# Column strips for the head, gates, energies and logits of a two-part transformer kernel, with its inputs queued between weight chunks

## The chip, the cores and the metric

The kernel runs on one core of a Trainium2 chip. The metric is the device time of one execution in microseconds (us). Everything is computed in 32-bit floats; the later layers use 32-bit products made of a high and a low part.

## What is computed

The reference takes 256 latent tokens `x` and 256 context tokens `ctx` of width 1024, and runs one block with a three-branch mixer and 16 experts, then four transformer layers. What the change touches lies in the first block:

```python
mod_l = jnp.split((jax.nn.silu(c) @ ada_w[l] + ada_b[l])[:, None, :], 6, axis=-1)
zc = modulate(rmsnorm(ctx, norm1_w[l]), mod_c[0], mod_c[1]) @ w_in[l] + b_in[l]
zl = modulate(rmsnorm(x, norm1_w[l]), mod_l[0], mod_l[1]) @ w_in[l] + b_in[l]
...
k = k * lax.rsqrt(jnp.sum(k * k, axis=0, keepdims=True) + EPS)      # filter energies
...
g_logits = (t @ lp["moe_rg_w"] + lp["moe_rg_b"]).astype(jnp.float32)
p_top, g_sel = lax.top_k(jax.nn.softmax(g_logits, axis=-1), 1)
e_logits = (t @ lp["moe_re_w"] + lp["moe_re_b"]).astype(jnp.float32).reshape(B * L, MOE_GROUPS, MOE_PER_GROUP)
...
a = jax.nn.silu(hg) * hu * combine[..., None].astype(t.dtype)
```

The slice `zc[..., OFF_MLG:OFF_GATE]` (and that of `zl`) of 16 columns holds the input and forget gates of the mLSTM branch.

## The kernel before

The order of the work is written out by hand for each engine; semaphores join the engines.

**Weights.** SyncE streams all weights through `ring`, 12 slots of 512 KB. Up to the experts they come as 31 chunks of four slots (2 MB), of which three fit; a chunk's load waits until `chunk_used` says that the chunk three earlier is done (L333). The signal rides on the first matmul after the chunk's last one (`used`). From the experts on (unit `split0`) they come as pairs of slots (1 MB), and each unit is split into `high` (ScalarE, L1143) and `low` (VectorE, L1592) before TensorE takes it; `split_to(n)` is the loop that does this up to unit n, and it stands in the order of both engines.

**Head.** ScalarE's queue loads `vecs`, `consts`, `xt` (the latents) and `ctx`, beside SyncE's chunks 0 to 2 and nine small loads of GpSimd. `ada(j)` multiplies one chunk of `ada_w` by the conditioning vectors in four column strips: weight tile k of 8 goes to the 32 output rows of strip k mod 4, so four matmuls of 32 columns each stand side by side in the array; `mod_out` copies the result to SBUF and `fold_columns` adds the four strips with a matmul against `fold`. Between `ada(1)` and `ada(2)` the mean square of all 512 tokens is taken with eight full matmuls (`mean_w`); VectorE forms the inverse root (L1598 to L1604) and scales both halves (L1606); `mods_ready` then lets ScalarE apply the modulation (L1172), and `in_values(0)` starts the projections. `in_values(s)` for s = 0 to 3 are the four value tiles, `in_keys(i)` the keys. Chunk 4 holds the value weights.

**Gates.** After `in_values(3)` the 16 gate columns are made for four token tiles, each with eight matmuls that stream 16 columns, and one for the bias. ScalarE copies them to `zp`, and after `in_keys(0)` TensorE turns them.

**Filter energies.** `energy(o)` for o = 0, 1 sums the squared filter taps with 16 matmuls of one column; VectorE takes them in `energy_eps`.

**Logits and expert 0.** After the second norm (`x_ready`) two token tiles of 20 logits are made with 18 matmuls. VectorE routes (L1982 to L2010; `first_hot` runs three times), then splits units 4 to 10, then makes expert 0's `hidden` (L2024), for which ScalarE's silu (L1425) is needed. TensorE runs `ffn_up(0)` meanwhile; `ffn_up(1)` waits for `h_raw`.

A matmul with 32-bit operands stands as two MATMUL records in the trace: eight matmuls are x16 there, and as x8 in the order rows below.

## Time and profile before

| What | us |
|---|---|
| median of three runs (2325.89 to 2328.65) | 2326.47 |
| the profiled execution, its own time | 2323.77 |
| its span on the core | 2322.0 |
| TensorE busy | 2149.4 (93%) |
| VectorE, ScalarE, GpSimd busy | 1280.7, 919.2, 109.0 |

### The profile page before, as it was taken

To read this page: it belongs to the slowest core of one execution; us is meant where nothing else is said; L and a number is where in the kernel's file an instruction comes from. 1 tells how busy PE (TensorE), PEld (TensorE's weight loads), DVE (VectorE), ACT (ScalarE), POOL (GpSimd) and SP (SyncE) were. 2 spreads that over 40 slices of the span, in tenths; PEclk is the share of its full clock that TensorE was granted. 3 is DMA by queue.
4 is the path that set the end of the run, shared out by engine and by line. 5 is a ranking of instruction groups with operands and counts; after the bars stand their busy time and mean duration, and the time that the engine had idled before them with its cause. 6 is when DMAs were issued, how large, how long until landed. Compare 5 with 4: busy or idle time off the path is not lost.

```text
span 2322.0 us, 27972 instructions
## 1 busy us (share of the span) xinstructions
PE 2149.4 (93%) x11510; PEld 1732.2 (75%) x11510; DVE 1280.7 (55%) x1903; ACT 919.2 (40%) x1448; POOL 109.0 (5%) x115
## 2 busy tenths in 40 slices
PE   4998999998999998899999998999998999988997
PEld 1556867775788877688799887788787788766886
DVE  1263742325555566555568676655576755656554
ACT  1123432003444435344345544444355444354442
POOL 1000000000000001000001012100001000020000
PEclk8799989998999999999999999999999999989999
DMA  7213334533454542345544332455543554424551
GB/s 291 85 66 152 122 140 147 194 137 117 162 181 181 182 164 108 136 181 183 173 182 171 128 126 93 145 183 182 179 146 128 181 181 181 163 94 152 181 181 73
DMA packets 47102, 357.23 MB, mean 154 GB/s; under 512 B 5370, under 2 KB 5557, under 8 KB 9664
## 3 DMA queue, kind: packets, MB, share of 16 engines
q1 hardware_dynamic: 41616, 334.51, 40.0%
q0 software_dynamic: 4784, 18.38, 2.3%
q10 hardware_dynamic: 576, 2.55, 0.3%
q8 instruction: 91, 1.49, 0.3%
q14 instruction: 35, 0.29, 0.0%
HBM read 354.38 MB, written 1.05 MB: 153 GB/s over the span
## 4 chain that ended last, share of the span: by engine, by line
PE 83%; DVE 10%; ACT 3%; issue 2%; DMA 1%; POOL 0%; ACTq 0%; DVEq 0%
PE pg L435 53%; PE pd L435 23%; PE pm L435 4%; DMA rh<-in_ctx 1%; PE pm L866 1%; DVE low L1592 1%; DVE small L1889 1%; DVE rs L1925 1%; DVE rs L1924 1%; DVE rs L1885 1%; DVE ar L2101 1%; DVE ar L1683 1%; ACT ar L1483 1%; PE pm L1008 1%; DVE xs L1935 0%
## 5 line engine op out<-in xcount | busy, mean ns | idle before, releaser
L1592 DVE TENSOR_TENSOR low<-ring,high 128x1024 fp32r<-128x1024 f32 x512 | 622.9, 1236 | 356.9 <-ACT high L1143 356.7
L435 PE MATMUL pg<-high,xs 128*128 128x512 f32 (+1 forms) x2496 | 749.6, 378 | 29.5 <-DVE xs L1935 14.3
L1143 ACT CAST high<-ring 128x1024 fp32r<-128x1024 f32 x512 | 525.1, 1048 | 372.7 <-PE pd L435 163.9
L435 PEld LDWEIGHTS pg<-high,xs 128*128 128x128 f32 x2496 | 464.2, 194 | 118.3 <-issue 21.3
L435 PE MATMUL pg<-low,xs 128*128 128x512 f32 (+1 forms) x1248 | 467.5, 375 | 0.0
L435 PE MATMUL pd<-high,hid 128*128 128x512 f32 x960 | 311.7, 396 | 7.0 <-DVE hid L2016 7.0
L435 PEld LDWEIGHTS pg<-low,xs 128*128 128x128 f32 x1248 | 242.5, 194 | 40.7
L435 PE MATMUL pg<-xs,high 128*128 128x256 f32 x1344 | 242.1, 283 | 0.0
L435 PEld LDWEIGHTS pd<-high,hid 128*128 128x128 f32 x960 | 180.7, 188 | 50.5 <-DVE hid L2016 8.2
L435 PEld LDWEIGHTS pg<-xs,high 128*128 128x128 f32 x1344 | 206.3, 188 | 5.0 <-issue 4.7
L435 PE MATMUL pg<-rh,ring 128*128 128x256 f32 (+1 forms) x832 | 207.4, 409 | 0.0
L435 PEld LDWEIGHTS pg<-rh,ring 128*128 128x128 f32 x832 | 161.3, 196 | 45.6 <-issue 25.3
L435 PE MATMUL pd<-low,hid 128*128 128x512 f32 x480 | 189.5, 395 | 0.0
L435 PE MATMUL pg<-xs,low 128*128 128x256 f32 x672 | 189.1, 281 | 0.0
L435 PEld LDWEIGHTS pg<-xs,low 128*128 128x128 f32 x672 | 126.5, 188 | 0.0
L435 PEld LDWEIGHTS pd<-low,hid 128*128 128x128 f32 x480 | 90.3, 188 | 20.9
L361 POOL TENSOR_TENSOR ar<-ar,small 128x256 f32<-128x256 f32 (+1 forms) x64 | 82.8, 1322 | 437.0 <-DVE small L2127 437.0
L2016 DVE TENSOR_TENSOR hid<-pm,hid 128x512 fp32r<-128x512 f32 x60 | 41.4, 691 | 93.6 <-ACT hid L1416 93.6
L1416 ACT CAST hid<-pm 128x512 fp32r<-128x512 f32 x60 | 35.2, 587 | 125.3 <-PE pm L866 125.3
L1483 ACT ACTIVATE ar<-ar,small 128x257 f32<-128x257 f32 (+5 forms) x128 | 67.0, 525 | 40.6 <-DVE small L2121 29.2
L1425 ACT ACTIVATE ar<-pg 128x256 f32<-128x256 f32 x120 | 46.2, 386 | 85.1 <-PE pg L435 85.0
L2081 DVE TENSOR_TENSOR ar<-ar,ropes 128x512 f32<-128x512 f32 x42 | 37.0, 880 | 68.4 <-ACT ar L1462 42.5
(322 smaller groups left out, 2048.9 us busy)
## 6 DMA issues: line engine op xcount, KB each, us to landing
ring<-in_wstream SPq DMA_DIRECT2D x256, 1024.0 KB, 4.8
ring<-in_wstream SPq DMA_DIRECT2D x31, 2048.0 KB, 7.8
gb<-in_long_rows POOLq DMA_DIRECT2D x21, 512.0 KB, 4.3
hdec<-in_hy_decay POOLq DMA_DIRECT2D x4, 512.0 KB, 4.4
rh<-in_xt ACTq DMA_DIRECT2D x1, 1024.0 KB, 23.1
rh<-in_ctx ACTq DMA_DIRECT2D x1, 1024.0 KB, 27.9
cx<-in_cx_tables POOLq DMA_DIRECT2D x1, 1024.0 KB, 5.1
cx<-in_dft_tables POOLq DMA_DIRECT2D x1, 1024.0 KB, 8.5
```

The source lines that it names most:

```text
L361: last = gp.tensor_tensor(w, w, smx[:, b, 2, t, 2 * p:2 * p + 2].unsqueeze(2).to_broadcast([P, 2, n]), ALU.mult)
L435: ins = nc.tensor.matmul(dst, lhs, rhs, start=start, stop=stop, skip_group_check=skip)
L866: last = nc.tensor.transpose(pm[u % 2][:, i * T + t * P:i * T + (t + 1) * P], hidden[:, t, i * P:(i + 1) * P], ident)
L1008: nc.tensor.transpose(pm[i][:, 0:P], scores(q, 0)[:, h, g * P:(g + 1) * P], ident)
L1143: nc.scalar.copy(high[:, (s - split0) % NHIGH, :], ring[:, s % NRAW, :]).then_inc(S("high_done"), 1)
L1416: nc.scalar.copy(hid[:, u % 2, 0, :, :], pm[u % 2][:, :].rearrange("p (i t) -> p i t", t=T)).then_inc(S("hid_high"), 1)
L1425: nc.scalar.activation(silu_g[:, t, :], pg[t][:, 0:T], ACT.Silu).then_inc(S("silu_done"), 1)
L1483: last = nc.scalar.activation(s, s, ACT.Exp, bias=smx[:, b, 0, t, h:h + 1], accum_out=smx[:, b, 1, t, h:h + 1])
L1592: V.tensor_tensor(low[:, s % NRAW, :], ring[:, s % NRAW, :], high[:, (s - split0) % NHIGH, :].bitcast(F32), ALU.subtract).then_inc(S("low_ ...
L1683: last = V.scalar_tensor_tensor(d, src, w[i], d, ALU.mult, ALU.add)
L2016: V.tensor_tensor(hid[:, u % 2, 1, :, :], pm[u % 2][:, :].rearrange("p (i t) -> p i t", t=T), hid[:, u % 2, 0, :, :].bitcast(F32), ALU.sub ...
L2081: V.tensor_tensor(rt[:, 0, :, :], raw[:, e % 2, :, :], cos.unsqueeze(1).to_broadcast([P, 2, T]), ALU.mult)
```

## The change

- **Input order.** The latents are loaded on SyncE's queue behind chunk 0, the context behind chunk 1, instead of on ScalarE's queue beside the chunks.
- **Head.** The mean squares are made by half, each in column strips (`square_strips`) and then folded by two full matmuls (`square_mean`) from a copy in SBUF; the latents' squares go to VectorE. The inverse root of each half is formed by itself, the latents' first; the context is scaled only after the modulation is ready. `ada(2)` and `ada(3)` write other PSUM banks. GpSimd sets the constants before its loads.
- **Gates, energies, logits.** The 128-token side is streamed (512 or 256 columns) and the narrow weights stand in four strips; ScalarE copies the result to SBUF (gates and logits with their bias), and a few narrow matmuls against `fold` add the strips and turn them. Between strips and fold other work is placed: `in_values(3)`, `in_pair("g", 0)`, `in_pair("g", 3)`, the first unit of `ffn_up(0)`.
- **Routing.** `first_hot` takes four VectorE instructions instead of eleven, with a constant `rank`.
- **Splits.** VectorE's split of the first four expert units stands ahead of the second norm instead of behind it; `hidden` and silu of expert 0 come after the split of unit 5 instead of unit 10.

```diff
+                if c == 0:
+                    sp.dma_start(rh[:, 0:2048], a["xt"]).then_inc(S("x_loaded"), 16)
+                elif c == 1:
+                    sp.dma_start(rh[:, 2048:4096], a["ctx"]).then_inc(S("ctx_loaded"), 16)
...
-            pe.wait_ge(S("consts_loaded"), 16)
+            def square_strips(half):
+
+                pe.wait_ge(S(("lat_sq", "ctx_sq")[half]), 1)
+                for k in range(KT):
+                    g = k % 4
+                    last = mm(pd[32 * g:32 * g + 32, 2, half * T:(half + 1) * T], ones[:, 0:32], sq2[:, half, k, :],
+                              k < 4, k >= 4)
+                last.then_inc(S("var_strips"), 1)
+
+            def square_mean(half):
+
+                pe.wait_ge(S("var_rows"), half + 1)
+                mm(pm[1][:, half * T:half * T + P], mean_w[:, :], nrm[:, 2, half * T:half * T + P], True, True)
+                mm(pm[1][:, half * T + P:(half + 1) * T], mean_w[:, :], nrm[:, 2, half * T + P:(half + 1) * T], True, True
+                   ).then_inc(S("nrm_var"), 1)
+
             pe.wait_ge(S("c_silu"), 1)
             ada(0, pg[0])
+            pe.wait_ge(S("ones_set"), 1)
+            square_strips(0)
             ada(1, pg[1])
+            square_mean(0)
+            pe.wait_ge(S("consts_loaded"), 16)
             fold_columns(0, pm[0][:, 0:8])
-            pe.wait_ge(S("constants"), 1)
-            pe.wait_ge(S("nrm_sq"), 2)
-            for k in range(KT):
-                last = mm(pm[1][:, :], mean_w[:, :], sq2[:, :, k, :], k == 0, k == KT - 1)
-            last.then_inc(S("nrm_var"), 1)
-            ada(2, pg[0])
+            square_strips(1)
+            ada(2, pd[:, 0, :])
+            square_mean(1)
             fold_columns(1, pm[0][:, 8:16])
-            pe.wait_ge(S("mod_row"), 2)
-            ada(3, pg[1])
+            ada(3, pd[:, 1, :])
             fold_columns(2, pm[0][:, 16:24])
             fold_columns(3, pm[0][:, 24:32])
+            pe.wait_ge(S("constants"), 1)
...
             mm(pm[1][0:64, 0:T], hyw[0:33, 0:64], feat, True, True).then_inc(S("hy_net"), 1)
             in_values(2)
+            for k in range(KT):
+                g = k % 4
+                last = mm(pm[0][32 * g:32 * g + 32, :], wg32[:, k, :], hc[:, :, k, :], k < 4, k >= 4)
+            last.then_inc(S("gate_strips"), 1)
             in_values(3)
+            pe.wait_ge(S("gates_copied"), 1)
             for s in range(4):
-                for k in range(KT):
-                    mm(pm[0][:, s * 16:(s + 1) * 16], hc[:, s // 2, k, (s % 2) * P:(s % 2 + 1) * P], wg16[:, k, :], k == 0, False)
-                last = mm(pm[0][:, s * 16:(s + 1) * 16], ones[0:1, :], row("b_gates", 0, 16), False, True)
+                last = mm(pm[0][:, s * 16:(s + 1) * 16], gate_rows[:, s * P:(s + 1) * P], fold[:, 0:16], True, True)
             last.then_inc(S("gates_raw"), 1)
...
                 pe.wait_ge(S("hy_tapsq"), o + 1)
+                if o:
+                    pe.wait_ge(S("hy_eps"), o)
+                for i in range(4):
+                    last = mm(pm[0][32 * i:32 * i + 32, :], ones[:, 0:32], hdec[:, i // 2, (i % 2) * DB:(i % 2 + 1) * DB],
+                              True, True)
+                last.then_inc(S("hy_energy"), 1)
+
+            def energy_columns(o):
+
+                pe.wait_ge(S("energy_copied"), o + 1)
                 for c in range(BT):
-                    for i in range(4):
-                        last = mm(pm[0][:, 4 * o + c:4 * o + c + 1],
-                                  hdec[:, i // 2, (i % 2) * DB + c * P:(i % 2) * DB + (c + 1) * P],
-                                  ones[:, 0:1], i == 0, i == 3)
-                last.then_inc(S("hy_energy"), 1)
+                    last = mm(pm[0][:, 4 * o + c:4 * o + c + 1], energy_rows[:, c * P:(c + 1) * P], fold[:, 0:1], True, True)
+                last.then_inc(S("hy_energies"), 1)
 
             def spectrum(o):
...
-            last.then_inc(S("logits"), 1)
+            for k in range(KT):
+                g = k % 4
+                last = mm(pm[0][32 * g:32 * g + 32, 0:T], wr32[:, k, :], h1[:, k, :], k < 4, k >= 4)
+            last.then_inc(S("logit_strips"), 1)
+
+            def logit_columns():
+
+                pe.wait_ge(S("logits_copied"), 1)
+                for s in range(TT):
+                    last = mm(pm[0][:, s * 20:(s + 1) * 20], logit_rows[:, s * P:(s + 1) * P], fold[:, 0:20], True, True)
+                last.then_inc(S("logits"), 1)
 
             def weights(n):
...
-                    ffn_up(u0, range(4))
+                    ffn_up(u0, (0,))
+                    logit_columns()
+                    ffn_up(u0, (1, 2, 3))
                 else:
...
+            def norm_root(half):
+
+                act.wait_ge(S("nrm_eps"), half + 1)
+                cols = slice(half * T, (half + 1) * T)
+                nc.scalar.activation(nrm[:, 1, cols], nrm[:, 0, cols], ACT.Sqrt).then_inc(S("nrm_root"), 1)
+
+            mod_out(0)
+            mod_out(1)
+            norm_root(0)
+            act.wait_ge(S("ctx_loaded"), 16)
+            nc.scalar.activation(sq2[:, 1, :, :], hc[:, 1, :, :], ACT.Square).then_inc(S("ctx_sq"), 1)
+            mod_out(2)
+            norm_root(1)
...
+            act.wait_ge(S("gate_strips"), 1)
+            nc.scalar.activation(gate_rows[:, :], pm[0][:, :], ACT.Identity, bias=vec("b_gates")
+                                 ).then_inc(S("gates_copied"), 1)
             take_values(3)
...
+            act.wait_ge(S("logit_strips"), 1)
+            nc.scalar.activation(logit_rows, pm[0][:, 0:T], ACT.Identity, bias=vec("b_route")
+                                 ).then_inc(S("logits_copied"), 1)
             act.wait_ge(S("group_diff"), 1)
...
-                    last.then_inc(S("nrm_scaled"), 1)
-            then(last)
+            dve.wait_ge(S("x_loaded"), 16)
+            V.tensor_tensor(sq2[:, 0, :, :], hc[:, 0, :, :], hc[:, 0, :, :], ALU.mult).then_inc(S("lat_sq"), 1)
+
+            def norm_rows(half):
+
+                cols = slice(half * T, (half + 1) * T)
+                dve.wait_ge(S("var_strips"), half + 1)
+                V.tensor_copy(nrm[:, 2, cols], pd[:, 2, cols]).then_inc(S("var_rows"), 1)
+                dve.wait_ge(S("nrm_var"), half + 1)
+                V.tensor_scalar(nrm[:, 0, cols], pm[1][:, cols], EPS_RMS, None, ALU.add).then_inc(S("nrm_eps"), 1)
+
+            def norm_scale(half):
+
+                cols = slice(half * T, (half + 1) * T)
+                dve.wait_ge(S("nrm_root"), half + 1)
+                y, v, t = (nrm[:, i, cols] for i in (1, 0, 2))
+                then(V.reciprocal(y, y))
+                then(V.scalar_tensor_tensor(t, y, -0.5, y, ALU.mult, ALU.mult))
+                then(V.tensor_tensor(t, t, v, ALU.mult))
+                then(V.scalar_tensor_tensor(y, t, 1.5, y, ALU.add, ALU.mult))
+                return V.tensor_tensor(hc[:, half, :, :], hc[:, half, :, :], y.unsqueeze(1).to_broadcast([P, KT, T]), ALU.mult)
+
+            norm_rows(0)
+            norm_scale(0).then_inc(S("nrm_scaled"), 1)
+            norm_rows(1)
...
+            dve.wait_ge(S("ctx_loaded"), 16)
+            then(norm_scale(1))
             for k in range(KT):
...
+            split_to(split0 + 3)
             dve.wait_ge(S("x_landed"), 16)
             for c in range(2):
...
             low_part(1, 0)
             normalised(1, 1)
             low_part(1, 1)
-            split_to(split0 + 3)
...
-                then(V.tensor_copy(seen, dst[:, :, 0:1]))
-                for j in range(1, 4):
-                    then(V.tensor_scalar(free, seen, -1.0, 1.0, ALU.mult, ALU.add))
-                    then(V.tensor_tensor(seen, seen, dst[:, :, j:j + 1], ALU.max))
-                    then(V.tensor_tensor(dst[:, :, j:j + 1], dst[:, :, j:j + 1], free, ALU.mult))
+                then(V.tensor_tensor(ranked, dst, rank.unsqueeze(1).to_broadcast([P, 2, 4]), ALU.mult))
+                then(V.tensor_reduce(seen, ranked, AX, ALU.max))
+                then(V.tensor_tensor(dst, ranked, wide(seen), ALU.is_equal))
 
             dve.wait_ge(S("logits"), 1)
             then(V.tensor_copy(R[:, 0:40], pm[0][:, 0:40]))
...
-                    first_by_tile = by_tile and u == u0
-                    if first_by_tile:
-                        hidden_raw(u, 0)
+                    if u == u0:
+                        if by_tile:
+                            hidden_raw(u, 0)
                         split_to(UP[u] + 5)
-                        hidden_raw(u, 1)
+                        for t in range(int(by_tile), TT):
+                            hidden_raw(u, t)
                     split_to(UP[u] + 8)
                     if u > u0:
                         hidden_low(u - 1)
                     split_to(UP[u] + 10)
-                    if not first_by_tile:
+                    if u > u0:
                         for t in range(TT):
                             hidden_raw(u, t)
                 last = u0 + n - 1
```

Three places show how the order moves. First TensorE's head, up to the first two value tiles (`pg`, `pd` and `pm` are PSUM, `rs` the squares, `rh` the tokens, `nrm` the rows of the norm). Before:

```order
L435 MATMUL pg<-ring,cs 32x512 x16
L435 MATMUL pm<-consts,mod_row 128x2 x4
L435 MATMUL pm<-rs,mean_w 128x512 x8
L435 MATMUL pg<-ring,cs 32x512 x8
L435 MATMUL pm<-consts,mod_row 128x2 x4
L435 MATMUL pg<-ring,cs 32x512 x8
L435 MATMUL pm<-consts,mod_row 128x2 x8
L435 MATMUL pg<-ring,rh 128x512 x8
```

Now:

```order
L443 MATMUL pg<-ring,cs 32x512 x8
L443 MATMUL pd<-rs,ones 32x256 x8
L443 MATMUL pg<-ring,cs 32x512 x8
L443 MATMUL pm<-nrm,mean_w 128x128 x2
L443 MATMUL pm<-consts,mod_row 128x2 x4
L443 MATMUL pd<-rs,ones 32x256 x8
L443 MATMUL pd<-ring,cs 32x512 x8
L443 MATMUL pm<-nrm,mean_w 128x128 x2
L443 MATMUL pm<-consts,mod_row 128x2 x4
L443 MATMUL pd<-ring,cs 32x512 x8
L443 MATMUL pm<-consts,mod_row 128x2 x8
L443 MATMUL pg<-ring,rh 128x512 x8
```

The latents' squares now come between the first two chunks of `ada_w`, and the eight full matmuls of 512 columns are gone.

Second, TensorE's gates, behind the third value tile (`wg` and `ar` the gate weights). Before:

```order
L435 MATMUL pg<-ring,rh 128x512 x8
L435 MATMUL pg<-rows,ones 128x512
L435 MATMUL pm<-wg,rh 128x16 x8
L435 MATMUL pm<-rows,ones 128x16
...
L435 MATMUL pm<-ar 64x256
L435 MATMUL pg<-rh,ring 128x512 x8
L435 MATMUL pm<-consts,zp 8x128 x16
```

Now:

```order
L443 MATMUL pm<-rh,ar 32x512 x8
L443 MATMUL pg<-ring,rh 128x512 x8
L443 MATMUL pg<-rows,ones 128x512
L443 MATMUL pm<-consts,gate_rows 128x16 x4
L443 MATMUL pm<-ar 64x256
L443 MATMUL pg<-rh,ring 128x512 x8
L443 MATMUL pm<-consts,zp 8x128 x16
```

Of 36 narrow matmuls in one place, 8 in strips stand ahead of the fourth value tile and 4 narrow ones behind it.

Third, VectorE between the routing and expert 1 (`low` is a split, `ar<-ar,pg` the hidden tile, `hid` its low part). Before:

```order
L1592 TENSOR_TENSOR low<-ring,high 128x1024 [waits high_done,combine]
L1592 TENSOR_TENSOR low<-ring,high 128x1024 [waits high_done] x6
L2024 SCALAR_TENSOR_TENSOR ar<-ar,pg 128x256 [waits silu_done] x2
L1592 TENSOR_TENSOR low<-ring,high 128x1024 [waits high_done] x2
L2016 TENSOR_TENSOR hid<-pm,hid 128x512 [waits hid_high]
```

Now:

```order
L1654 TENSOR_TENSOR low<-ring,high 128x1024 [waits high_done,combine]
L1654 TENSOR_TENSOR low<-ring,high 128x1024 [waits high_done]
L2097 SCALAR_TENSOR_TENSOR ar<-ar,pg 128x256 [waits silu_done] x2
L1654 TENSOR_TENSOR low<-ring,high 128x1024 [waits high_done] x7
L2089 TENSOR_TENSOR hid<-pm,hid 128x512 [waits hid_high]
```

Five splits have gone from ahead of the hidden tile to behind it.

## Rows read from the trace of the kernel before

**Rows 1.** The page: the chain that ended last, by engine.
```profile
PE 83%; DVE 10%; ACT 3%; issue 2%; DMA 1%; POOL 0%; ACTq 0%; DVEq 0%
```

**Rows 2.** Chain that ended last, to the first projection: start us, us, what.
```profile
2.14 27.92 DMA rh<-in_ctx
30.08 3.71 ACT rs L1153 x2
...
50.41 3.36 DVE nrm L1601
...
58.19 2.30 DVE rh L1606
...
61.95 18.05 PE pg L435 x36
```

**Rows 3.** Stretches: length, PE, PEld, DVE, ACT, POOL busy, PEclk, DMA share, GB/s.
```profile
4.00:14.00 10.00, 0.00 (x0) 0.00 (x0) 0.00 (x0) 0.92 (x2) 2.86 (x10) 1.00 1.02 416
66.00:96.00 30.00, 30.00 (x69) 12.08 (x68) 4.75 (x14) 3.98 (x6) 1.59 (x3) 1.00 0.19 70
97.00:111.00 14.00, 14.00 (x74) 13.49 (x73) 0.00 (x0) 0.78 (x5) 0.00 (x0) 0.60 0.43 151
558.00:570.00 12.00, 12.00 (x45) 10.95 (x46) 7.55 (x26) 0.27 (x2) 0.00 (x0) 0.50 0.48 176
```

**Rows 4.** TensorE in order of time, modulation chunks: start us, us, tiles, count.
```profile
16.73 5.81 PE L435 MATMUL pg<-ring,cs 128*32 128x512 f32 x32 [16.73 <-DMA consts<-in_consts]
...
167.44 1.92 PE L435 MATMUL pm<-ring,cs 128*32 128x512 f32 x16
169.30 7.17 PE L435 MATMUL pg<-rh,ring 128*128 128x256 f32 x32
...
195.15 3.64 PE L435 MATMUL pm<-ring,cs 128*32 128x512 f32 x16
```

**Rows 5.** TensorE in order of time, gates and the work around them.
```profile
80.50 7.13 PE L435 MATMUL pg<-ring,rh 128*128 128x512 f32 x16
...
96.73 1.96 PE L435 MATMUL pm<-wg,rh 128*128 128x16 f32 x16
...
111.53 9.71 PE L435 MATMUL pg<-rh,ring 128*128 128x512 f32 x16
121.16 3.66 PE L435 MATMUL pm<-consts,zp 128*8 128x128 f32 x32
```

**Rows 6.** TensorE in order of time, the two filter energies.
```profile
308.14 6.99 PE L435 MATMUL pm<-ones,hdec 128*128 128x1 f32 x32 [2.73 <-ACT hdec L1332]
...
316.69 9.54 PE L435 MATMUL pg<-rh,ring 128*128 128x256 f32 x32
326.07 8.75 PE L435 MATMUL pd<-hk,cx 128*128 128x512 f32 x20
...
355.24 3.63 PE L435 MATMUL pm<-ones,hdec 128*128 128x1 f32 x32
...
369.31 8.75 PE L435 MATMUL pd<-hk,cx 128*128 128x512 f32 x20
```

**Rows 7.** TensorE in order of time, logits and the first expert.
```profile
557.54 3.60 PE L435 MATMUL pm<-wr,ar 128*128 128x20 f32 x16 [4.18 <-DVE xs L1935]
...
585.70 0.80 PE L435 MATMUL pg<-high,xs 128*128 128x512 f32 x1 [6.32 <-DVE ar L2024]
```

**Rows 8.** Chain that ended last, in expert 1: start us, us, what.
```profile
594.49 5.57 PE pg L435 x24
```

**Rows 9.** VectorE in order of time, routing and the first hidden tiles.
```profile
565.79 0.20 DVE L1982 COPY ar<-pm 128x40 f32<-128x40 f32 x1 [3.77 <-PE pm L435]
...
577.22 8.04 DVE L1592 TENSOR_TENSOR low<-ring,high 128x1024 fp32r<-128x1024 f32 x7
585.17 0.87 DVE L2024 SCALAR_TENSOR_TENSOR ar<-ar,pg 128x256 f32<-128x256 f32 x2
```

**Rows 10.** ScalarE in order of time, the same place.
```profile
581.93 1.28 ACT L1425 ACT_TABLE_LOAD   x1
```

More of the change, by code:

```diff
@@ L469, in fold_columns @@
                 for i in range(4):
[L470 removed]
+                    last = mm(dst[:, 2 * i:2 * i + 2], mod_row[:, j % 2, i * P:(i + 1) * P], fold[:, 0:2], True, True)
                 last.then_inc(S("mod_folded"), 1)
@@ L2282, in constants @@
     put("flip", np.eye(P)[::-1])
-    fold = np.zeros((P, 2))
-    for g in range(4):
-        fold[32 * g, 0] = fold[32 * g + 1, 1] = 1.0
-    put("fold", fold)
+    put("fold", np.tile(np.eye(32), (4, 1)))
+    put("rank", np.tile(np.arange(4, 0, -1), (P, 1)))
     ch = 2 * np.pi * np.outer(p, p) / P
```

94 lines of the change are left out of this document (41 added, 53 removed).

## The prediction

> **What bounds the kernel now.** I read the page first, then the chain that ended last, then TensorE in order of time at the places that the change touches. The chain is TensorE for 83% of the span [rows 1], so a microsecond taken out of TensorE's own queue is a microsecond of the span, wherever no other engine is about to finish later. The change touches four places, all before expert 1.
>
> *Head.* The first projection starts at 61.95 [rows 2]. Up to there the chain is no work of TensorE: the context lands at 30.1 (27.9 after its issue), both halves are squared (1.85 each), the root of 512 columns is inverted (3.36), both halves are scaled (2.30 each) [rows 2]. In that time the DMA engines move 416 GB/s [rows 3]: the inputs are late because they share the engines with three, in the end four, 2 MB chunks.
>
> *Gates.* From 96.73 to 121.16 TensorE makes the gates, a small matmul and `in_keys(0)`: 24.4 us [rows 5]. Of it 13.8 are the gates, 72 records that stream 16 columns. They begin at 0.12 each and end at 0.22, the granted clock of the stretch is 0.60 [rows 3], and `in_keys(0)` takes 9.71 where such a block takes 7.13 at full pace [rows 5]: the narrow matmuls are paid twice.
>
> *Energies.* The same: the 32 one-column records of the first energy take 6.99, 0.22 each, the pace at which the gates ended, and the pair behind it 9.54; the whole from 308.14 to `spectrum(0)` at 326.07 is 17.9. The second, 355.24 to 369.31, is 14.1 [rows 6].
>
> *Logits and expert 0.* `x_ready` comes at 557.5; the logits take 8.1 at 0.50 [rows 3, 7]; VectorE then routes for 11.4 (565.79 to 577.22), splits seven units (8.0) and makes the hidden tile, and `ffn_up(1)` starts at 585.70 after an idle 6.3 [rows 7, 9]. Its first records are slow again (0.80 for the first [rows 7]); later ones take 5.57 for 24, 0.23 each [rows 8].
>
> **The price of a strip block.** `ada` is one already: 16 records of 512 columns start at 167.44 and the next work at 169.30, 1.86 in all; at half clock 3.64 [rows 4]. So eight matmuls of 512 columns cost 1.86 at 2.4 GHz, about 3.6 at 1.2; four cost 0.93; eight of 256 columns 0.93 and 1.8. A fold is eight narrow records of 0.12, 0.95; at half clock 1.9 [rows 5].
>
> **Head, step by step.** On SyncE's queue the order is now chunk 0, `xt`, chunk 1, `ctx`, chunk 2. I take the measured 416 GB/s from 2 us on, 1.0 MB for the small loads, and first come first served within the queue: `xt` is complete at 12 (4.1 MB), chunk 1 at 17, `ctx` at 20, chunk 2 at 25, chunk 3 at 30, chunk 4 (the value weights) at 35 (13.6 MB). `chunk_used` is now raised by the square strips and means, but each comes at least 4 us before the queue runs dry, so no load waits.
> TensorE at half clock, as before at the start: `ada(0)` 10 to 13.6; VectorE squares the latents from 12 to 14.3 (2.3, the scaling's row), strips to 16.5; `ada(1)` 17.4 to 21; mean, eps, then ScalarE's table load (1.28 [rows 10]) and root to 23.3; ScalarE squares the context (1.85) to 25.2; strips to 27, `ada(2)` to 30.5. VectorE scales the latents from 23.4 (1.7 for 256 columns instead of 3.36, three short steps, 2.3) to 28.7, under that. Mean and fold to 33, `ada(3)` to 36.7, copy, two folds, the modulation's small steps: the first projection at 41.5. With all behind 27 at full clock it is 35.5, and then chunk 4 (35) is as late. I take 40, near the slow end, since TensorE idles or runs narrow folds for about a third of this time: **22 less** (bounds 14 and 26.5).
> A rule of the skill gives the input order another price. The Trainium skill, "DMA: Bandwidth & Descriptors", section "Queues, rings and completion order", says that each DMA engine takes the queues in turn, packet by packet; with equal turns the context, 2.6 MB deep in its own queue, would have come at about 15 and the move behind chunk 1 would delay it by 5. The row says 30.1, so the sum goes by the row.
>
> **Gates.** Strips 1.86, folds 0.95, the small matmul 0.57, `in_keys(0)` 7.13: 10.5 for 24.4. ScalarE's copy is covered by `in_values(3)` (8 us); without that cover it would cost 0.6. **13.9 less**; at half clock throughout 8.
>
> **Energies.** Strips 0.93, the narrow fold of `fold_columns` 0.95, the pair 7.1, the new fold 0.95: 9.9 for 17.9. But TensorE still idles 2.7 before it [rows 6], so I leave 1.8 of half pace in: 6.2 less (bounds 3 and 8). Second: 0.93, `ada(8)` 1.9, pair 7.1, 0.95 for 14.1: 3.2 less (0 and 3.5). VectorE now gets its energies a pair later and is held there in `energy_eps`; behind it wait `add_columns` and the next convolution. `ada(7)`, which needs the former, comes only after `spectrum(0)` (8.75), so this costs nothing. **9.4 less.**
>
> **Logits and expert 0.** From `x_ready`: strips at half clock 1.8, the first unit's 12 records at twice 0.23, 5.2 (I take 5.1), folds 0.5, logits ready at 7.5 (now 8.2). Routing loses 21 of its 57 instructions, each 0.20 (11.43 / 57): 7.3 for 11.4, to 14.9. Two splits of 1.2 instead of seven (8.04 / 7 = 1.15), hidden tile 0.45: `ffn_up(1)` at 17.8, where now it is 28.2. TensorE itself is through `ffn_up(0)` at 15.7 (36 more records of 0.23), and ScalarE's silu, behind two casts (2.1) and the table load (1.28), comes at 16.7, just under VectorE. So it idles 2.1 instead of 6.3 and should keep its pace, some ten records at 0.23 saved, 2.3 more. The four splits put ahead of the norm fall into idle time of VectorE; the 4.6 they took ran beside the logits. **12.7 less** (9 and 14).
>
> **Sum.** 22 + 13.9 + 9.4 + 12.7 = 58. Nothing behind expert 1 is touched and DMA is far from full there, so all of it shows: span 2322.0 - 58 = 2264.0, with the 1.8 outside the span 2265.8; the median of the runs is 2.7 above the profiled execution, so **2268.5**. Bounds: 14 + 8 + 3 + 9 = 34 less (2292) and 26.5 + 13.9 + 11.5 + 14 = 66 less (2260).
>
> **Rivals.**
> - *All at full pace* (0.15): the denser head rouses the clock from `ada(2)` on, the idle before the energy costs nothing. Head 26.5, energies 11.5: 65 less, **2262**. Against it, each idle of over 2 us so far was followed by slow matmuls.
> - *The hand-offs decide the head* (0.18): each half now goes TensorE, VectorE, TensorE, VectorE, ScalarE, VectorE in turn, and one late step (the copy for the second mean waits behind the scaling of the latents) pushes `ada(3)` and all after it. First projection at 50: **2279**.
> - *The clock stays low at the new places* (0.11): gates save 8, energies 3, the expert 5: 38 less, **2288**.
> - *Strips don't stand side by side* (0.04): each record costs its full 0.43. Gates +5, energies +5, logits +5, squares +10: **2293**. The `ada` rows speak against it. A switch of the array's form could also cost by itself: the Trainium skill, "TensorEngine Tiling (Array Packing)", section "Key Properties", says that changing the tiling mode drains the engine. It gives no price; the `ada` row holds both of its switches, 0.15 over four groups of 0.43, so six new blocks pay 1 us by the row, and the prices above have it in.
> - *Slower* (0.01): the half clock of the start lasts through the projections, because the head's dense matmuls of 512 columns are replaced by strips and idle between them. A block of 7.1 us then takes 14.2; from the ninth such block on the gain of 58 is gone, and nine make 2268.5 + 64 = **2332**. Against it, the projections that start at 61.95, after a head in which VectorE alone works for ten microseconds, are at clock 1.00 from 66 on [rows 2, 3].
>
> **How the numbers follow.** The forecast has 0.51. The range may leave out at most 0.2: it drops the three dearest cases (0.16 together), holds the hand-off case at 2279 with some room, and at the low end the full-pace case at 2262 with five for what the four prices may add up to beyond it: 2257 to 2285. A measurement tells about 0.2% (4.7 us) from no change; every case but the last is more than six times that below 2326.5: faster 0.98, same 0.01, slower 0.01.
>
> **What would show it.** In the changed profile: first projection near 40; gates, strips to `zp` without the value tile, about 10.5, at clock 1.00; `in_keys(0)` at 7.1; `spectrum(0)` 10 to 12 after the energy's start; `ffn_up(1)` 18 after the second norm, with an idle of 2. I am wrong in the head if `ctx` lands after 25 or the first projection comes after 45, and in the rest if the small folds alone pull the clock down, or if a new wait on `energy_copied`, `gates_copied` or `logits_copied` stands in TensorE's list.

## The result and the profile after

| | before | after |
|---|---|---|
| median of the runs, us | 2327.39 (2325.89 to 2328.65, 4 runs) | 2267.98 (2265.89 to 2268.92, 4 runs) |
| the profiled execution: own time, span | 2323.77, 2322.0 | 2268.92, 2267.1 |

The ratio is 0.9744, 95% interval 0.9727 to 0.9761: 59.4 us or 2.6% faster. Predicted were 2268.5 with a range of 2257 to 2285. The same pair was timed again for e12 below: 2265.65 against 2319.04, ratio 0.977 (0.9752 to 0.9789), 53.4 us. So the changed kernel repeats to 2.3 us, and the kernel before moved by 8.4: the gain is 53 to 59 us.

The page of the changed kernel, the engines' busy time and the chain by engine:

```profile
PE 2121.1 (94%) x11438; PEld 1701.7 (75%) x11438; DVE 1281.1 (57%) x1890; ACT 920.1 (41%) x1452; POOL 109.2 (5%) x115
...
PE 85%; DVE 9%; ACT 3%; issue 1%; DMA 1%; POOL 0%; SPq 0%; DVEq 0%; ACTq 0%
```

Beside [rows 1], TensorE has 85% of the chain instead of 83%, and of its busy time 28 us have gone. To see where the time went I read the same marks in both traces, the start of a stage on TensorE, in us:

| mark | before | after | less by then |
|---|---|---|---|
| first projection | 62.0 | 39.4 | 22.6 |
| gates turned (`zp`) | 121.2 | 84.4 | 36.8 |
| first energy | 308.1 | 271.1 | 37.0 |
| `spectrum(0)` | 326.1 | 284.1 | 42.0 |
| `spectrum(1)` | 369.3 | 324.0 | 45.3 |
| logits | 557.5 | 514.0 | 43.5 |
| expert 0's hidden tile turned | 593.9 | 537.1 | 56.8 |
| end of the span | 2322.0 | 2267.1 | 54.9 |

The stretch of the last line but one to the end, 1728 us, holds nothing that the change touches. Over the fourteen profiled executions of this study it lasted 1722 to 1732 us, and the edits below don't touch it either, so the total of one execution carries several microseconds of scatter that a mark does not. I read the experiments by the marks up to the turned hidden tile. A mark comes from one execution, though, and two stretches ahead of that tile also vary where no edit touches them: from the first projection to `zp` 45.0 or 46.8 to 48.2 us, and from the logits to the turned tile 21.6 to 21.8 or 23.0 to 23.1 (see the last section).

**Head.** TensorE in order of time (start, us, operation, tiles, counts, idle before and its releaser), to be held against [rows 2]:

```profile
9.71 3.64 PE L443 MATMUL pg<-ring,cs 128*32 128x512 f32 x16 [9.71 <-ACT cs L1191]
15.46 1.94 PE L443 MATMUL pd<-rs,ones 128*32 128x256 f32 x16 [2.10 <-DVE rs L1660]
19.81 3.64 PE L443 MATMUL pg<-ring,cs 128*32 128x512 f32 x16 [2.41 <-DMA ring<-in_wstream]
...
27.68 1.93 PE L443 MATMUL pd<-rs,ones 128*32 128x256 f32 x16 [1.58 <-ACT rs L1212]
29.39 3.29 PE L443 MATMUL pd<-ring,cs 128*32 128x512 f32 x16
...
34.04 1.92 PE L443 MATMUL pd<-ring,cs 128*32 128x512 f32 x16
...
39.39 2.90 PE L443 MATMUL pg<-ring,rh 128*128 128x512 f32 x3 [1.55 <-ACT rh L1220]
```

The context no longer decides. TensorE starts at 9.7 instead of 16.7, since it no longer waits for `consts` ahead of `ada(0)`, and then waits 2.1 us for the latents' squares, 2.4 for chunk 1, 1.6 for the context's squares and 1.6 for the modulation. The last of the four `ada` chunks is the first at full pace (1.92 for 16 records, before it 3.64, 3.64, 3.29).

**Gates.** The same view, in answer to [rows 5]:

```profile
65.79 1.92 PE L443 MATMUL pm<-rh,ar 128*32 128x512 f32 x16
67.64 7.13 PE L443 MATMUL pg<-ring,rh 128*128 128x512 f32 x16
...
75.76 1.06 PE L443 MATMUL pm<-consts,gate_rows 128*128 128x16 f32 x8
...
77.32 7.13 PE L443 MATMUL pg<-rh,ring 128*128 128x512 f32 x16
84.39 3.66 PE L443 MATMUL pm<-consts,zp 128*8 128x128 f32 x32
```

**Energies.** Both up to their spectra, in answer to [rows 6]:

```profile
271.10 1.94 PE L443 MATMUL pm<-hdec,ones 128*32 128x512 f32 x8 [2.73 <-ACT hdec L1383]
272.96 1.87 PE L443 MATMUL pm<-consts,mod_row 128*128 128x2 f32 x8
274.69 8.76 PE L443 MATMUL pg<-rh,ring 128*128 128x256 f32 x32
...
284.10 8.83 PE L443 MATMUL pd<-hk,cx 128*128 128x512 f32 x20
...
313.44 1.06 PE L443 MATMUL pm<-hdec,ones 128*32 128x512 f32 x8
...
323.97 6.25 PE L443 MATMUL pd<-hk,cx 128*128 128x512 f32 x14
```

**Logits and expert 0.** TensorE, in answer to [rows 7], then VectorE, in answer to [rows 9]:

```profile
513.99 1.93 PE L443 MATMUL pm<-ar,wr 128*32 128x256 f32 x16 [4.18 <-DVE xs L2010]
...
520.76 0.52 PE L443 MATMUL pm<-consts,ar 128*128 128x20 f32 x4
...
531.37 0.50 PE L443 MATMUL pg<-high,xs 128*128 128x512 f32 x1 [1.64 <-DVE ar L2097]
```

```profile
521.31 0.20 DVE L2055 COPY ar<-pm 128x40 f32<-128x40 f32 x1 [7.38 <-PE pm L443]
...
528.57 2.36 DVE L1654 TENSOR_TENSOR low<-ring,high 128x1024 fp32r<-128x1024 f32 x2
530.84 0.87 DVE L2097 SCALAR_TENSOR_TENSOR ar<-ar,pg 128x256 f32<-128x256 f32 x2
```

From the logits' first record to `ffn_up(1)` it is 17.4 us instead of 28.2, and the idle before it 1.64 instead of 6.32. VectorE has two splits (2.36) between the routing and the hidden tile, not seven. The stretches of the places above, with the columns of [rows 3]:

```profile
4.00:14.00 10.00, 3.64 (x16) 0.59 (x16) 0.98 (x1) 0.80 (x2) 2.62 (x8) 1.00 1.02 378
66.00:76.00 10.00, 10.00 (x36) 3.76 (x29) 0.00 (x0) 1.61 (x4) 0.00 (x0) 1.00 0.01 2
272.00:284.00 12.00, 12.00 (x56) 9.76 (x48) 2.37 (x4) 2.38 (x4) 1.14 (x2) 0.75 0.68 264
516.00:528.00 12.00, 12.00 (x46) 9.68 (x47) 5.55 (x35) 3.53 (x6) 0.00 (x0) 0.82 0.68 252
```

The gates now run at 1.00 where [rows 3] had 0.60. At the energy and the logits part of the slow clock has stayed (0.75 and 0.82).

### The profile page after: what moved, and what is told of

It is laid out like the page before. It is cut to its first block, busy times and chain, and to the rows that moved or that the text cites. A ratio compares the mean times of both kernels' runs of the same rounds, so it can differ in the third digit from the quotient of the medians.

```text
span 2267.1 us, 27822 instructions
## 1 busy us (share of the span) xinstructions
PE 2121.1 (94%) x11438; PEld 1701.7 (75%) x11438; DVE 1281.1 (57%) x1890; ACT 920.1 (41%) x1452; POOL 109.2 (5%) x115
## 4 chain that ended last, share of the span: by engine, by line
PE 85%; DVE 9%; ACT 3%; issue 1%; DMA 1%; POOL 0%; SPq 0%; DVEq 0%; ACTq 0%
PE pg L443 55%; PE pd L443 24%; PE pm L443 2%; PE pm L908 1%; DVE small L1964 1%; DVE low L1654 1%; DMA ring<-in_wstream 1%; DVE rs L2000 1%; DVE rs L1999 1%; DVE rs L1960 1%; DVE ar L2175 1%; DVE ar L1758 1%; ACT ar L1545 1%; PE pm L1052 1%; DVE xs L2010 1%
## 5 line engine op out<-in xcount | busy, mean ns | idle before, releaser
L1545 ACT ACTIVATE ar<-ar,small 128x257 f32<-128x257 f32 (+5 forms) x128 | 67.0, 525 | 41.5 <-DVE small L2195 30.1
L1486 ACT ACTIVATE ar<-pg 128x256 f32<-128x256 f32 x120 | 46.2, 386 | 84.5 <-PE pg L443 84.4
```

The lines of the kernel that those rows point to most:

```text
L1486: nc.scalar.activation(silu_g[:, t, :], pg[t][:, 0:T], ACT.Silu).then_inc(S("silu_done"), 1)
L1545: last = nc.scalar.activation(s, s, ACT.Exp, bias=smx[:, b, 0, t, h:h + 1], accum_out=smx[:, b, 1, t, h:h + 1])
```

## The experiments

Twelve kernels ran, in three groups, each on one chip with the kernel before beside them. The medians of before were 2320.7 in the first group (e1 to e4), 2325.2 in the second (e5 to e8) and 2319.0 in the third (e9 to e12). Only the third group holds the changed kernel (e12). For e2 to e8 the cost against the changed kernel is therefore read from marks: their medians lie 4.4 to 10.6 us above 2267.98, their ratios 0.0033 to 0.0073 above 0.9744 (7.7 to 17 us), and the base that moved by 8 us makes both rough.

The theory is the prediction's: four separate gains, the head's in the waits ahead of the first projection, the others in TensorE's own queue, with the clock as a good part of them at the gates, the energies and the expert. The rivals stand with each run: that one part of the head is the whole of it, or that narrow matmuls cost what they cost for another reason.

### The head: order alone, split alone

e1 puts only the input order into the kernel before; e2 takes only the order out of the changed kernel.

```diff
+                if c == 0:
+                    sp.dma_start(rh[:, 0:2048], a["xt"]).then_inc(S("x_loaded"), 16)
+                elif c == 1:
+                    sp.dma_start(rh[:, 2048:4096], a["ctx"]).then_inc(S("x_loaded"), 16)
...
-            act.dma_start(rh[:, 0:2048], a["xt"]).then_inc(S("x_loaded"), 16)
-            act.dma_start(rh[:, 2048:4096], a["ctx"]).then_inc(S("x_loaded"), 16)
```

> The kernel before with one edit: latents and context on SyncE's queue behind chunks 0 and 1, head and all else as before. Theory A (late inputs are half of the head's cost, the whole-width norm the other half): context at 20 instead of 30.1, squares to 24.4, the eight full matmuls to 34, then 16 us of norm as before: first projection at about 50 instead of 61.95, the kernel 12 us faster than before (2315). Theory B (the order of the inputs is the whole of the head's gain): first projection near 40, 22 us faster. Theory C (the split norm is the whole of it): within 3 us of before.

> The changed kernel with the two input loads back on ScalarE's queue beside the chunks; everything else as changed. Theory A: the latents land at 22 instead of 13, TensorE stands at the square strips behind ada(0), ada(1) starts at 26 instead of 19.8, first projection at about 46 instead of 39.4: 6.5 us slower than the changed kernel (4 to 10). Theory B: 20 us or more slower. Theory C: no difference.

e1: 2313.85 us (2309.23 to 2321.71, 10 runs), ratio 0.9969 (0.9949 to 0.9989). Its chain that ended last begins with the context, which lands at 21.9 instead of 30.1 (start, us, what):

```profile
2.12 19.79 DMA rh<-in_ctx
...
21.93 3.71 ACT rs L1155 x2
...
52.72 7.47 PE pg L439 x10
```

The first projection comes at 52.7, 9.2 earlier than before. Of it 8.2 is the context's landing. Theory A had said 50 and 12 us: its parts are right, its size was too large, and by medians e1 is only 6.9 us under before. Theories B (40) and C (within 3 us) are out.

e2: 2275.62 us (2274.08 to 2276.76, 4 runs), ratio 0.9799 (0.9767 to 0.983). TensorE's head:

```profile
26.86 1.93 PE L439 MATMUL pd<-rs,ones 128*32 128x256 f32 x16 [13.91 <-DVE rs L1658]
...
46.33 8.80 PE L439 MATMUL pg<-ring,rh 128*128 128x512 f32 x16 [1.55 <-ACT rh L1218]
```

Now the latents land at 24.4, and TensorE idles 13.9 us for their squares. The first projection comes at 46.3, 6.9 later than in the changed kernel (expected: 6.5). So of the head's 22.6 the order is worth 9.2 in the old head and 6.9 in the new one, and all the rest together 13.4 to 15.7: neither is the whole. This rest is the split norm with its strips, the squares on VectorE, the two other PSUM banks, and `ada(0)` without the wait for `consts`; these were not taken apart. Both loads stood in ScalarE's queue behind 0.46 MB of `vecs` and `consts`. The latents landed 22.7 us after their issue and the context 24.4 after its own, but `consts`, ahead of both, had itself taken 14.4.

The Trainium skill, "DMA: Bandwidth & Descriptors", section "Queues, rings and completion order", has each DMA engine take the queues in turn, packet by packet. The prediction's estimate of 15 us from it, for data 2.6 MB deep, takes turns of equal size. The packets are not equal: ScalarE's queue moved its first 0.47 MB in 288 packets, SyncE's has 8 KB in each. An estimate from the same rule with turns of one packet is about 22 us for the context: its 576 packets (2.6 MB), as many of SyncE's (4.6 MB) and 1.0 MB of small loads at 416 GB/s. It landed at 30.1 in [rows 2] and at 26.5 here, so neither estimate agrees.

### The gates: back, and spread

e3 makes the gates as before, 72 narrow records behind `in_values(3)`. e4 makes the same records, but one token tile behind each of the four value tiles (`gate_tile(s)` is the loop of before for tile s). In both, ScalarE's copy for the strips is gone.

```diff
...
             in_values(0)
+            gate_tile(0)
             in_values(1)
+            gate_tile(1)
...
             in_values(2)
-            for k in range(KT):
-                g = k % 4
-                last = mm(pm[0][32 * g:32 * g + 32, :], wg32[:, k, :], hc[:, :, k, :], k < 4, k >= 4)
-            last.then_inc(S("gate_strips"), 1)
+            gate_tile(2)
             in_values(3)
...
+            gate_tile(3).then_inc(S("gates_raw"), 1)
```

> The changed kernel with the gates as before: 72 narrow records in one place behind the fourth value tile, nothing else undone. Theory A: 14 us slower than the changed kernel (2282), the narrow matmuls falling to 0.22 each and in_keys(0) at 9 to 10 us. Theory B (the gain at the gates was the earlier context or another piece of the head): under 5 us.

> As the one before, but each token tile's 18 narrow records stand behind its own value tile instead of all 72 together. Same matmuls, same number. Theory A (nearly half of the gates' cost was the fallen clock, which needs the narrow matmuls in a row): 0.12 each throughout, in_keys(0) at 7.1, so 72 x 0.12 = 8.8 for 2.8: 6 us slower than the changed kernel (2274), 8 us faster than with the gates in one place. Theory D (the cost belongs to the narrow matmuls wherever they stand): 14 us slower.

e3 (gates as before): 2278.55 us (2277.01 to 2284.85, 4 runs), ratio 0.9817 (0.9782 to 0.9851). From the first projection to `zp` it is 59.1 us instead of 45.0, 14.1 more. Six kernels that leave this part as it is (e2, e5 to e8, e11) took 46.8 to 48.2 for it, against which it is 10.9 to 12.3 more:

```profile
73.90 1.96 PE L443 MATMUL pm<-ar,rh 128*128 128x16 f32 x16
...
76.11 2.82 PE L443 MATMUL pm<-ar,rh 128*128 128x16 f32 x16
...
79.39 3.60 PE L443 MATMUL pm<-ar,rh 128*128 128x16 f32 x16
...
88.55 9.85 PE L443 MATMUL pg<-rh,ring 128*128 128x512 f32 x16
```

Sixteen narrow records take 1.96, then 2.82, then 3.60: the pace halves while they run, and `in_keys(0)` behind them pays 2.7. Theory B (under 5 us) is out.

e4: 2275.85 us (2272.2 to 2287.26, 4 runs), ratio 0.9808 (0.9768 to 0.9849). The same stretch takes 59.4. By this mark spreading gave nothing, and by medians 2.7 us, within the scatter of both:

```profile
58.94 1.96 PE L443 MATMUL pm<-ar,rh 128*128 128x16 f32 x16
...
61.72 8.83 PE L443 MATMUL pg<-ring,rh 128*128 128x512 f32 x16
...
71.53 2.17 PE L443 MATMUL pm<-ar,rh 128*128 128x16 f32 x16
...
74.17 9.99 PE L443 MATMUL pg<-ring,rh 128*128 128x512 f32 x16
...
88.78 9.51 PE L443 MATMUL pg<-rh,ring 128*128 128x512 f32 x16
```

The narrow records now stay near full pace (1.96 and 2.17 for 16), but from the second such run on the dense tile behind it loses: 8.83, 9.99 and 9.51 instead of 7.13, together 6.9 us, at a granted clock of 0.80, 0.71 and 0.74. The narrow records themselves, with their bias, cost 6.8 more than the strips and folds. So theory A's 6 us failed, and theory D's 14 held. Where it lies is new: here half of the loss falls on the dense work behind the narrow records. The first such run (at 48.6) cost nothing behind it. In strips, the 16 records of 512 columns (1.92) are followed by a value tile of 7.13 in all ten traces that have them. Behind the eight folds of 16 columns (1.06) `in_keys(0)` takes 7.13 in four of these and 8.56 to 8.83 in six, so up to 1.7 of e4's last 2.4 may not be the narrow records'.

### The energies back

`energy(o)` is one function for both energies. With it `energy_columns` and ScalarE's two copies go:

```diff
...
-                if o:
-                    pe.wait_ge(S("hy_eps"), o)
-                for i in range(4):
-                    last = mm(pm[0][32 * i:32 * i + 32, :], ones[:, 0:32], hdec[:, i // 2, (i % 2) * DB:(i % 2 + 1) * DB],
-                              True, True)
+                for c in range(BT):
+                    for i in range(4):
+                        last = mm(pm[0][:, 4 * o + c:4 * o + c + 1],
+                                  hdec[:, i // 2, (i % 2) * DB + c * P:(i % 2) * DB + (c + 1) * P],
+                                  ones[:, 0:1], i == 0, i == 3)
```

> The changed kernel with both filter energies as before: 32 one-column records each, no copy, no fold. Theory A: 4.9 + 3.5 = 8.5 us slower than the changed kernel, energy(0) to spectrum(0) back at about 18 us, energy(1) to spectrum(1) at 11 to 14. Theory B (the gain there is only the clock's phase): under 3 us.

e5: 2277.82 us (2274.54 to 2279.66, 4 runs), ratio 0.9796 (0.9773 to 0.9818). From the first energy to `spectrum(0)` 18.1 instead of 13.0, from the second to `spectrum(1)` 14.1 instead of 10.5: 8.6 in all, as expected (8.5), and theory B (under 3) is out. One thing goes the other way: the output projection, far behind both, takes 27.73 us here and 29.43 in the changed kernel, which leaves 6.9 net.

### Routing, hidden tile, logits, each back alone

e6 gives `first_hot` its eleven instructions back, e7 puts expert 0's silu and hidden tile behind unit 10, e8 makes the logits with 18 narrow matmuls ahead of the expert. Of e7, VectorE's list (ScalarE's silus move in the same way):

```diff
...
-                    if u == u0:
-                        if by_tile:
-                            hidden_raw(u, 0)
+                    if u == u0 and by_tile:
+                        hidden_raw(u, 0)
                         split_to(UP[u] + 5)
-                        for t in range(int(by_tile), TT):
-                            hidden_raw(u, t)
+                        hidden_raw(u, 1)
                     split_to(UP[u] + 8)
...
-                    if u > u0:
+                    if u > u0 or not by_tile:
```

> The changed kernel with first_hot as before, 21 more VectorE instructions of 0.20 in the routing. Theory A (VectorE's chain sets when expert 1 starts): 4.2 us later all through, TensorE's idle before ffn_up(1) 5.8 instead of 1.6, and as many as ten slow records behind it: 4 to 6.5 us slower. Theory E (TensorE and ScalarE's silu would have come as late anyway): under 1.5 us.

> The changed kernel with silu and hidden of expert 0 behind the split of unit 10 again. Theory A: five splits of 1.15 = 5.7 us ahead of the hidden tile, idle 7.4 before ffn_up(1), slow records behind it: 6 to 8 us slower. Theory E: under 1.5 us, since the splits are needed before long anyway.

> The changed kernel with the logits as before (36 narrow records in one place, VectorE's short routing and early hidden kept). Theory A: logits at 8.2 after the norm instead of 7.3, and TensorE through ffn_up(0) 6 us later (at 22 instead of 15.5), so TensorE becomes the later one and ffn_up(1) starts at 22 instead of 17.4: 4.5 us slower. Theory E (VectorE alone decides): 0.9 us slower.

`ffn_up(1)` in e6, then in e7; in the changed kernel the idle is 1.64 and the first record takes 0.50:

```profile
537.49 0.80 PE L443 MATMUL pg<-high,xs 128*128 128x512 f32 x1 [5.81 <-DVE ar L2099]
```

```profile
539.51 0.79 PE L443 MATMUL pg<-high,xs 128*128 128x512 f32 x1 [7.33 <-DVE ar L2095]
```

| | median, ratio | by marks |
|---|---|---|
| e6 | 2272.38 (2269.92 to 2277.7), 0.9777 (0.9753 to 0.9801) | `ffn_up(0)` to the turned tile 27.7 for 21.2: 6.5 |
| e7 | 2277.54 (2269.34 to 2281.34), 0.9791 (0.9763 to 0.982) | the same 28.6: 7.4 |
| e8 | 2273.91 (2271.91 to 2278.32), 0.9787 (0.9761 to 0.9812) | logits to the turned tile 27.4 for 23.1: 4.3 |

All three came as theory A had it (4 to 6.5, 6 to 8 and 4.5); theory E is out for each. The medians of e6 and e8 are 4.4 and 5.9 us above 2267.98, that of e7 9.6. Each can hold the 1.4 us by which the logits' stretch varies (last section), which changes none of these verdicts. Singly they cost 18.2, together they gave 13.3 (10.8 to `ffn_up(1)` and 2.5 behind it). They lie on the same chain, and the first two each make the idle long enough (5.8 and 7.3) for the slow first records (0.80 and 0.79 instead of 0.50) to come back.

### What the changed kernel left: two idles

The changed kernel still idles 2.73 us before the first energy (above), and 5.19 before the mLSTM's first scores, where all 28 records up to 162 run at half pace:

```profile
152.66 3.78 PE L443 MATMUL pd<-ar 128*128 128x256 f32 x8 [5.19 <-ACT ar L1305]
...
158.37 3.64 PE L443 MATMUL pm<-ring,cs 128*32 128x512 f32 x16
```

Both come from the order in which the engines' lists are written. e9 moves the first energy's strips behind the pair that followed them, and their fold behind `spectrum(0)`; ScalarE's copy and VectorE's `energy_eps(0)` move back with them. e10 moves ScalarE's three silus ahead of its copy of the output gate's pair, and the two for the keys wait for the second signal of the convolutions instead of the fourth. e11 does both; e12 is the changed kernel once more. TensorE's part of e9, then e10:

```diff
...
-            energy(0)
...
             in_pair("g", 0)
-            energy_columns(0)
+            energy(0)
             spectrum(0)
+            energy_columns(0)
```

```diff
...
             take_pair("o", 0)
+
+            act.wait_ge(S("conv_out"), 2)
+            nc.scalar.activation(kf, kf, ACT.Silu)
+            nc.scalar.activation(kc, kc, ACT.Silu)
+            act.wait_ge(S("conv_out"), 4)
+            nc.scalar.activation(qf, qf, ACT.Silu).then_inc(S("qk_silu"), 1)
             take_pair("o", 1)
-
-            act.wait_ge(S("conv_out"), 4)
-            nc.scalar.activation(qf, qf, ACT.Silu)
-            nc.scalar.activation(kf, kf, ACT.Silu)
-            nc.scalar.activation(kc, kc, ACT.Silu).then_inc(S("qk_silu"), 1)
```

> The changed kernel, with the first energy's strips moved two steps back in TensorE's order: the weights of the next half, the fold of chunk 6 and the pair before it stand ahead of them, so that ScalarE's squared taps (hdec), for which TensorE idled 2.73 us, are there when they are asked for. My theory: the idle of 2.7 goes, and with it the half clock that lasts 8.6 + 1.7 + 1.9 us behind it, of which about 3 us is loss: 5 to 6 us less than the changed kernel, and from the start of the first energy to spectrum(0) no record at half pace. Rival: the taps' chain through ScalarE and VectorE is what decides, and the wait only moves to the next hand-off (hy_eps before spectrum(0), or hy_energies): then the gain is 0 to 2 us, and an idle stands in front of spectrum(0) or the second taps.

> The changed kernel, with ScalarE's silu of the mLSTM's queries and keys moved ahead of its copy of the output gate's pair, in front of which it stands in no dependence. TensorE idled 5.2 us before the mLSTM's first scores, for these silus, and its first records after that were at half pace (about 3.8 us of loss). My theory: both go, 7 to 9 us less than the changed kernel. Rival: VectorE's convolution is the later of the two inputs of the silu; then moving the silu only moves ScalarE's own idle, and the gain is under 2 us.

> Both edits together on the changed kernel. My theory: they lie over 20 us apart and each removes an idle and the slow clock behind it, so they add: 12 to 15 us less than the changed kernel, about 2255 if it stands at 2268. Rival: a busier stretch is paid for by a slower clock elsewhere, so the sum is less than the two single gains by 3 us or more.

> The changed kernel once more, unchanged, in the same call as its three variants. It gives them their base, and it shows how much one part varies by itself: from the first projection to the turned gates the changed kernel took 45.0 us in its first profiled execution, and 46.8 to 48.2 in five variants that did not touch this part, with in_keys(0) at 8.6 to 8.8 us instead of 7.13. If that is variation from one execution to the next, this one may show 45 to 48; if the variants caused it, it shows 45.0 and in_keys(0) 7.13 again.

| | median of 4 runs, us | ratio to before | turned hidden tile at | against e12: mark, median |
|---|---|---|---|---|
| e12 | 2265.65 (2263.49 to 2267.73) | 0.977 (0.9752 to 0.9789) | 536.8 | |
| e9 | 2259.84 (2257.05 to 2260.86) | 0.974 (0.9724 to 0.9757) | 528.8 | -8.0, -5.8 |
| e10 | 2263.62 (2253.48 to 2271.33) | 0.9756 (0.9717 to 0.9795) | 527.3 | -9.5, -2.0 |
| e11 | 2251.15 (2247.47 to 2253.4) | 0.9703 (0.9685 to 0.9722) | 521.5 | -15.3, -14.5 |

e9, TensorE around the first energy:

```profile
270.06 7.17 PE L443 MATMUL pg<-rh,ring 128*128 128x256 f32 x32 [0.72 <-DMA ring<-in_wstream]
277.16 1.06 PE L443 MATMUL pm<-hdec,ones 128*32 128x512 f32 x8
278.15 8.85 PE L443 MATMUL pd<-hk,cx 128*128 128x512 f32 x20
286.84 0.95 PE L443 MATMUL pm<-consts,energy_rows 128*128 128x1 f32 x8
```

No record is slow, and the energy costs 1.06 and 0.95. What is late next is a transfer, 0.72 us of weights before the pair. From the taps' matmuls ahead of the first energy (255.7 in the changed kernel) to `spectrum(1)` it is 63.0 us against 68.3, 5.3 less, inside the 5 to 6 expected. The rest of the 8.0 came later: 1.7 in the output projection, which I had not foreseen, and 1.4 behind the logits. That 1.4 is no gain of this edit, since e2, e3 and e5, which leave both places alone, show it too.

e10, the same place as above:

```profile
147.61 1.89 PE L443 MATMUL pd<-ar 128*128 128x256 f32 x8
...
150.49 1.92 PE L443 MATMUL pm<-ring,cs 128*32 128x512 f32 x16
```

The idle is gone and every record is at full pace: from `zp` to the scores 5.4 less (62.9 against 68.3), from there to the filter taps 4.6 less, together somewhat more than the 7 to 9 expected. The mark at the turned tile says 9.5, the median only 2.0. The four runs do not agree among themselves (two near 2255, two near 2271) and only the first has a trace, so the silus' gain is shown up to the turned tile of that execution, and how much of it every execution keeps is open.

e11 is the fastest kernel of the study, 14.5 us under e12 and 3% under before. In the traces the two edits add: 5.4 and 4.6 at the silus, 5.7 at the energy and 1.7 in the output projection, as if each were alone. By medians 5.8 and 2.0 don't make 14.5, which is e10's scatter again.

e12 repeats the changed kernel's marks to within 0.3 us up to the turned tile, and then ends 5.4 earlier. From the first projection to `zp` it shows 45.0 us and `in_keys(0)` at 7.13, which both readings in its expectation allow. e9 and e10, at 45.0 and 45.1, speak against a variant as such being the cause of 46.8 to 48.2; it stays open.

## Why the prediction was right

The forecast case came in: 2267.98 against 2268.5. That the two agree to 0.5 us is luck. The span came 3.1 us longer than forecast (2267.1 against 2264.0), and the sum then added 2.7 because the median of before lay that much above its profiled execution; this time the median lies 0.9 below it. By terms, in the profiled executions:

| term | predicted | measured |
|---|---|---|
| head | 22 | 22.6 |
| gates | 13.9 | 14.2 |
| first energy | 6.2 | 4.9 |
| second energy | 3.2 | 3.5 |
| logits to `ffn_up(1)` | 10.4 | 10.8 |
| `ffn_up(1)` at full pace | 2.3 | 2.5 |
| parts that the sum left out | 0 | -3.6 |
| sum, span | 58 | 54.9 |

*Head.* Right in size, through two errors that cancel. Chunk 1 landed at 19.8, not 17: the stretch from 4 to 14 moved 378 GB/s, not the 416 that I took over from [rows 3], which accounts for 1 us of it. That put `ada(1)` 2.4 later and the context's squares after it. Against it `ada(3)` was already at full pace (1.92, not 3.6), where my 40 lay between the sum's two ends. The hand-off rival (2279) did not come: TensorE waits four times, three of them at a hand-off, but 1.6 to 2.4 us each, and `ada(3)` starts at 34.0 without a wait. e1 and e2 show that the order and the rest of the head both carry it.

*Gates.* As worked out: 1.92, 1.06, 0.64 and 7.13. ScalarE's copy is covered. e3 takes 14.1 back, 10.9 at the least. What the runs add is that spreading the narrow records doesn't keep the slow clock away (e4): half of their price was then paid by the tiles behind them. The prediction's sign of being wrong, small folds that alone pull the clock down, is neither met nor excluded: in six of ten traces `in_keys(0)` behind the folds lost 1.4 to 1.7, and in the same six the first value tile, after the head, had been slower too (8.80 to 10.1 against 8.59 to 8.67).

*Energies.* The term that was mis-sized: 9.4 forecast, 8.5 measured. I left 1.8 us of half pace behind the 2.7 idle. It was more: the strips took 1.94 for 0.93 to 1.06, the fold 1.87 for 0.95 and the pair 8.76 for 7.17, 3.4 us in all. The clock rose later than I took from the rows of before. In e9 the idle and the loss go together. e9 also moves the fold away, but at the silus e10 takes out only the idle, and the slow records behind it go too. With the 1.70 us of the output projection, which comes and goes with this edit (last section), the energies gave 6.8.

*Logits and expert 0.* Each step within 0.5 us of its place: strips 1.93 (1.8), logits ready at 7.3 (7.5), splits from 14.6 (14.9), `ffn_up(1)` at 17.4 (17.8), idle 1.64 (2.1). TensorE keeps its pace over this idle, as predicted, and does not over 5.8 (e6). That the four splits ahead of the norm cost nothing shows in the unchanged 4.18 before the logits.

*Parts that the sum left out.* I took nothing for them. The output projection's 64 records took 29.43 us, where before and in e9 they took 27.73. The remaining 1.9 lies in the scatter of the last 1728 us.

One reading of the prediction is wrong: not every idle of over 2 us was followed by slow matmuls. Before, the output projection started after an idle of 2.10 and ran at full pace, 27.73 for 64 records.

*The rivals.* Full pace everywhere (2262) was wrong at the energy and at the logits' first unit (clock 0.75 and 0.82). The clock staying low (2288) was wrong at the gates. Strips that don't stand side by side are excluded by 1.92 for 16 records of 512 columns (0.43 each would make 6.9), and a slow clock through the projections by the 7.13 at 67.64.

## What to carry to other kernels

A narrow matmul costs twice: a record of 16 columns took 0.12 us, as much as one of 512 columns does where four strips run side by side, and dense work behind such records ran at a lower clock. Turning the product round, so that the long side streams and the narrow weights stand in four column strips, took 14 of 24 us away (11 at the least), while spreading the same narrow records between dense tiles took next to nothing. After such a change look for the idles that are left on TensorE: those of 2.7 and 5.2 us here cost about as much again in slow records behind them (3.4 and 4.6), both were a matter of the order in the engines' lists, and together they gave 14.5 us more.

## What the runs showed of the hardware that was not expected

- The slow clock need not fall on the narrow records. In e4 they stayed at 0.12 to 0.14 us each and the dense tile behind them took 9.99 us for 7.13.
- The column of the granted clock does not tell everything. In the head `ada(0)` takes 3.64 us for 16 records, twice the 1.92 of `ada(3)`, in a stretch where the column says 1.00. The pace there is read from the records.
- The same program can have another clock in one execution than in another. e10's four runs took 2256.7, 2270.6, 2253.5 and 2271.3 us at a mean granted clock of 0.971, 0.964, 0.972 and 0.963.
- One place can run at two paces while nothing near it differs. `in_keys(0)`, behind the four folds of the gates, took 7.13 in the changed kernel, e12, e9 and e10, and 8.56 to 8.83 in e2, e5 to e8 and e11. In e11:

```profile
75.92 1.06 PE L443 MATMUL pm<-consts,gate_rows 128*128 128x16 f32 x8
...
77.49 8.83 PE L443 MATMUL pg<-rh,ring 128*128 128x512 f32 x16
```

- From the logits to the turned hidden tile it is 23.0 to 23.1 us in the changed kernel, e12, e4, e10 and e11, and 21.6 to 21.8 in e2, e3, e5 and e9, with the same order there. In the latter the half pace behind the strips ends about 1.4 us earlier.
- A slow spot can hang on an edit far away. The output projection's 64 records, after an idle of 2.10 in all fourteen traces, take 29.43 us in the nine whose first energy stands in strips ahead of the pair (the changed kernel, e12, e2 to e4, e6 to e8 and e10). They take 27.73 in the five others: before, e1 and e5 with one-column records, e9 and e11 with the strips behind the pair. The energy lies 190 us earlier. The changed kernel, then e9:

```profile
471.71 29.43 PE L443 MATMUL pd<-ring,rh 128*128 128x512 f32 x64 [2.10 <-DVE rh L1950]
```

```profile
466.57 27.73 PE L443 MATMUL pd<-ring,rh 128*128 128x512 f32 x64 [2.10 <-DVE rh L1950]
```

What carries it from the one place to the other was not tried, and the cause of all three differences is open.
